# One-hot sorting of token slots in f32 from the unsplit x, with unrolled experts and a third up-projection buffer

## The reference

```python
gate = jnp.sum(jax.nn.one_hot(e_idx, N_EXPERTS, dtype=jnp.float32) * w[..., None], axis=1).astype(x.dtype)
y = jnp.zeros_like(t)
for e in range(N_EXPERTS):
    h = jax.nn.silu(t @ w_gate[e]) * (t @ w_up[e])
    y = y + gate[:, e:e + 1] * (h @ w_down[e])
```

## Time and profile before

| | |
|---|---|
| median of 3 runs | 1006.26 us (1005.80 to 1006.55) |
| profiled execution, own time | 1011.19 us |
| its span, first to last instruction | 1009.4 us |
| mean granted clock of PE | 0.903 of full speed |
| PE busy | 809.6 us, 80% of the span |
| DVE, ACT, POOL busy | 343.1, 199.6, 57.4 us |
| read from HBM | 249.46 MB |

### The profile page before, as it was taken

How to read it: one execution, slowest core, us unless ns; L and a number is a source line. 1 busy time by engine, 2 the same in 40 slices (tenths; PEclk the granted TensorE clock), 3 DMA queues, 4 the chain that set the end, 5 groups by cost and what they waited for, 6 DMA issues and landing times.

```text
span 1009.4 us, 10730 instructions
## 1 busy us (share of the span) xinstructions
PE 809.6 (80%) x4044; PEld 409.5 (41%) x4048; DVE 343.1 (34%) x744; ACT 199.6 (20%) x477; POOL 57.4 (6%) x54
## 2 busy tenths in 40 slices
PE   6989999938897877878799997697499878777750
PEld 4656777435432222222344865455343222222210
DVE  1033444376122212122540137536722222121228
ACT  1213334140211101011210036612221111010111
POOL 1020000040000000000200000002300000000010
PEclk9987999958999999999989997798599999999985
DMA  9641009340599999999693643234055999999942
GB/s 361 195 149 84 1 1 410 133 167 20 193 398 425 429 427 425 430 425 424 228 405 109 238 195 139 74 136 167 1 209 233 428 426 430 426 425 428 424 158 89
DMA packets 41303, 264.02 MB, mean 262 GB/s; under 512 B 6168, under 2 KB 10974, under 8 KB 23600
## 3 DMA queue, kind: packets, MB, share of 16 engines
q1 hardware_dynamic: 32032, 243.95, 58.9%
q0 software_dynamic: 3328, 10.51, 3.5%
q10 hardware_dynamic: 5904, 9.04, 2.5%
HBM read 249.46 MB, written 14.01 MB: 261 GB/s over the span
## 4 chain that ended last, share of the span: by engine, by line
PE 50%; DMA 27%; DVE 12%; SPq 6%; ACT 3%; issue 2%; POOL 0%; ACTq 0%; DVEq 0%; POOLq 0%
DMA arena<-in_expert_w_up 25%; PE bank L824 15%; PE bank L766 5%; PE bank L1061 4%; PE bank L1076 3%; PE bank L838 3%; PE bank L817 3%; SPq L435 2%; PE bank L754 2%; PE bank L702 2%; PE bank L617 1%; DVE arena L1635 1%; PE bank L747 1%; DVE arena L1798 1%; PE bank L680 1%
## 5 line engine op out<-in xcount | busy, mean ns | idle before, releaser
L824 PE MATMUL bank<-arena 128*64 128x512 f32 x1024 | 246.9, 638 | 64.1 <-DMA arena<-in_expert_w_up 59.6
L824 PEld LDWEIGHTS bank<-arena 128*64 128x64 f32 x1024 | 77.8, 145 | 230.3 <-issue 187.2
L1723 DVE COPY arena<-bank 128x256 f32<-128x256 f32 x32 | 13.6, 425 | 350.2 <-PE bank L831 350.2
L838 PE MATMUL bank<-arena 128*64 128x512 f32 x512 | 116.9, 598 | 17.0 <-DVE arena L1723 17.0
L1269 ACT ACTIVATE arena<-bank 128x256 f32<-128x256 f32 x32 | 12.3, 384 | 286.6 <-PE bank L824 286.6
L838 PEld LDWEIGHTS bank<-arena 128*64 128x64 f32 x512 | 34.1, 136 | 77.7 <-issue 59.3
L1716 DVE RECIPROCAL arena<-arena 128x256 f32<-128x256 f32 x32 | 56.1, 1754 | 1.1
L766 PE MATMUL bank<-arena 128*128 128x512 f32 x128 | 55.4, 593 | 1.3 <-ACT arena L1135 1.3
L1061 PE MATMUL bank<-arena 128*128 128x512 f32 x96 | 43.7, 616 | 1.7 <-issue 0.9
L1295 ACT COPY arena<-bank 128x512 f32<-128x512 f32 x32 | 18.8, 587 | 110.1 <-PE bank L838 110.1
L610 PE MATMUL bank<-arena 128*128 128x128 f32 (+1 forms) x144 | 24.5, 334 | 16.4 <-DVE arena L1635 8.1
(11 more groups left out here) (253 smaller groups left out, 929.2 us busy)
## 6 DMA issues: line engine op xcount, KB each, us to landing
arena<-in_expert_w_gate SPq DMA_DIRECT2D x32, 2048.0 KB, 16.7
arena<-in_expert_w_up SPq DMA_DIRECT2D x32, 2048.0 KB, 21.2
arena<-in_expert_w_down SPq DMA_DIRECT2D x64, 1024.0 KB, 20.4
arena<-in_w_out SPq DMA_DIRECT2D x4, 2048.0 KB, 9.9
expert_rows<-arena ACTq DMA_DIRECT2D x64, 128.0 KB, 7.6
arena<-in_w_kv_shared SPq DMA_DIRECT2D x3, 2048.0 KB, 10.4
arena<-in_w_mem_kv SPq DMA_DIRECT2D x2, 2048.0 KB, 16.5
arena<-in_w_in_b SPq DMA_DIRECT2D x2, 2048.0 KB, 20.3
```

Source lines behind the costliest of these rows:

```text
L824: last = mm(bank[j][64 * half:64 * half + 64, :].rearrange("p (u f) -> p u f", u=2), slots[:, k, 0:CAP], w[:, :, k, 256 * half:256 * half ...
L838: last = mm(bank[3 + j][64 * n:64 * n + 64, :], hid_t[:, j, c, 64 * half:64 * half + 64], dn[j][:, half, c, 512 * n:512 * n + 512], start= ...
```

## The change

- `x_part`, `x_stack`, `x_rest`, `x_mid`, the rounding on ACT and the six subtractions on POOL go. POOL keeps one memset of the tail of `xs`.
- DVE makes two f32 one-hot matrices. `pick` (128 columns) holds experts 0 and 1, made from each token's place within those two experts right after the counts are copied. `sort_pick` (576 columns) holds all slots and is made later in the chain, as `pick` was.
- `pack_first` sorts the slots of experts 0 and 1: 24 f32 matmuls of 128 columns (eight blocks, three token tiles). ACT copies them straight into `xg`, and up 0 and up 1 follow each other.
- `turn_rows` sorts all 576 slots in nine turns over three banks: eight turns of 512 columns (three f32 matmuls each) and a ninth with the last 64 columns of all eight blocks (24 matmuls). Four turns stand between down 0 and down 1, five between down 1 and up 2. ACT copies the even turns out, DVE the odd ones.
- The three up buffers rotate, so U(e+3) is issued when up e is done; D(e+1) is issued when down e-1 is done.
- The loops over experts are written out. `keep_warm` before the sort goes from 1536 columns to 512.

```diff
@@ -218,19 +218,15 @@
-        x_part = zm.cut(3 * D).bitcast(BF16).rearrange("p (s t d) -> p s t d", s=3, t=2)
-        x_stack = zm.cut(D // 2).bitcast(BF16)
-        ln2_par = Region(part_at).cut(2, D)
+        sort_pick = zm.cut(3, PACK)
+        zm.cut(3 * D - 3 * PACK)
+        pick = zm.cut(3, 2 * CAP)
...
+        ups = [gu[0], gu_one, gu[1]]
...
@@ -478,34 +481,24 @@
+                load_up(l, 2, ups[2], up_in[2])
+                for e in range(NE):
+                    if e + 3 < NE:
+                        sp.wait_ge(up_done, NE * l + e + 1)
+                        load_up(l, e + 3, ups[e % 3], up_in[e % 3])
+                    if 1 <= e < NE - 1:
+                        sp.wait_ge(down_done, NE * l + e)
+                        load_down(l, e + 1, (e + 1) % 2, dn_in[(e + 1) % 2])
...
+            def pack_first(l):
+
+                for half in range(2):
+                    b = bank[5 + half]
+                    for k in range(4):
+                        for t, (a, n) in enumerate(TOKS):
+                            last = mm(b[:, 2 * CAP * k:2 * CAP * (k + 1)], x_tok[0:n, t, 4 * half + k::KC], pick[0:n, t, :],
+                                      start=t == 0, stop=t == 2)
+                    last.then_inc(packed, 1)
+
+            def turn_rows(l, which):
+
+                for i in which:
+                    if i == 0:
+                        pe.wait_ge(sort_ready, l + 1)
+                    if i < 3:
+                        pe.wait_ge(pack_taken, 2 * (l + 1))
+                    else:
+                        pe.wait_ge(*turn_taken(l, i - 3))
+                    b = bank[5 + i % 3]
+                    for k in range(1 if i < KC else KC):
+                        for t, (a, n) in enumerate(TOKS):
+                            if i < KC:
+                                last = mm(b[:, :], x_tok[0:n, t, i::KC], sort_pick[0:n, t, 0:512], start=t == 0, stop=t == 2)
+                            else:
+                                last = mm(b[:, CAP * k:CAP * (k + 1)], x_tok[0:n, t, k::KC], sort_pick[0:n, t, 512:PACK],
+                                          start=t == 0, stop=t == 2)
+                    last.then_inc(rows_turned, 1)
...
-                keep_warm(bank[1], 1536)
...
+                keep_warm(bank[1], 512)
+                pe.wait_ge(pick_ready, l + 1)
+                pack_first(l)
+                up(0)
+                up(1)
+                down(0)
+                turn_rows(l, range(FIRST_TURNS))
+                down(1)
+                turn_rows(l, range(FIRST_TURNS, TURNS))
+                up(2)
+                for e in range(3, NE):
+                    up(e)
+                    down(e - 1)
+                down(NE - 1)
...
@@ -1273,61 +1267,66 @@
+                for half in range(2):
+                    ac.wait_ge(packed, 2 * l + half + 1)
+                    for j in range(2):
+                        last = nc.scalar.copy(xg[:, j, 4 * half:4 * half + 4, :],
+                                              bank[5 + half][:, :].rearrange("p (k s) -> p k s", k=4)[:, :, CAP * j:CAP * (j + 1)])
+                        own(last, pack_taken if j else None)
+                gate(0)
+                gate(1)
+                store(0)
+                take_rows(range(FIRST_TURNS))
+                store(1)
+                take_rows(range(FIRST_TURNS, TURNS))
...
+                for i in (TURNS - 2, TURNS - 1):
+                    ac.wait_ge(*turn_taken(l, i))
+                take(2)
+                take(3)
+                gate(2)
+                take(4)
...
@@ -1679,7 +1661,13 @@
+                    out_of(V.tensor_copy(counts[:, 3 * NE:4 * NE], b[:, 3 * NE:4 * NE]))
+                own.settle()
+                for t, (a, n) in enumerate(TOKS):
+                    for e in range(2):
+                        c = NE * t + e
+                        own(ts(pick[0:n, t, CAP * e:CAP * (e + 1)], cst("iota")[0:n, 0:CAP], counts[0:n, c:c + 1],
+                               sel_any[0:n, c:c + 1], ALU.is_equal, ALU.mult), pick_ready if (t, e) == (2, 1) else None)
...
+                form(0)
+                turned(0)
+                form(1)
+                take_rows(range(FIRST_TURNS))
+                turned(1)
+                take_rows(range(FIRST_TURNS, TURNS))
+                form(2)
...
@@ -1888,28 +1884,14 @@
-                        own(G.tensor_tensor(r, x_tok[:, t, :], x_part[:, 0, t, :], ALU.subtract), rest_ready)
...
+                own(G.memset(xs[:, :, PACK:XGW], 0.0), tail_ready)
+                po.wait_ge(rows_turned, TURNS * (l + 1))
                 ln_load(ln2_par, "ln2_g", "ln2_b", l)
```

## The result

The median is 1077.67 us (1070.87 to 1082.83, 4 runs) against 1006.40 for the kernel before in the same comparison: a ratio of 1.0683, 95% interval 1.0589 to 1.0776. The prediction had 1018.0 in a range of 1007 to 1026. So the direction was right and the size was not: 71 us for 12. The profiled execution took 1082.04 us, its span 1080.2.

What follows compares the result with a forecast made beforehand. The weight stream bounds the mixture, with a hole before it and PE's tail after. A 7.5 us earlier start a layer, less a longer hole and tail, sums to +11.7 us: 1006.26 becomes 1018.0 us, range 1007 to 1026.

Steps and rivals of the forecast that it cites:

- the price of the sorts' records: pack_first, ninth turn: 0.11 us a record at full clock; wide turns: 0.433 us a record, 10.4 us for four turns.
- the 0.5 us that the prediction had allowed for the clock: In pack_first: 0.5 us added because PE's clock may rise later, within 6.4 us in all.
- The 32-row records: In turn_rows: a third of the wide records, with 32 rows only, priced in full like 128-row ones.
- narrow records leave PE at 1.2 GHz: Rival, chance 0.07: pack_first costs 4.2 us more, the ninth turn 5.3, time 1037 us.
- The wide f32 records are cheaper: Rival in turn_rows: under 0.433 us, at 0.22 each 997.6 us; chance 0.12 with other shortenings of PE's way to U5.
- the 32-row records cost in proportion: Rival in turn_rows, chance 0.08: 5.2 us less a layer, 1007.6 us, no change that can be told.
- The contention: POOL's subtractions slow three DVE operations between x and the ranks; removing them saves 7.48 us per layer.
- D3 behind U5: On SP's queue: D3 waits behind up 2 and U5 until about 295 us, though down 1 has long been done.
- the stream itself: Weight loads: U5 lands 12.8 us after its issue, U15 153.5 us later, an expert every 15.35 us.
- D13 behind U15: Layer's end: down 13 waits for D13, landing at 466.5 us, and stands before up 15; PE ends at 488.15.
- The passing of all delay before U5 to the end: Mixture's end is the start of gapless loads, plus loads still to come, plus PE's tail.
- the new order with its third buffer: Weight loads: the third buffer moves one U ahead of the hole and no D, leaving 11 U and 13 D.

Runs made afterwards that it cites:

- e5: Changed kernel with both edits: sorts read neighbouring columns of x and the third tile uses all 128 rows; 1028.88 us, ratio 1.0188.
- e1: Changed kernel with sorts reading 128 neighbouring columns of x instead of every eighth; 1055.89 us, ratio 1.0483.
- e2: Changed kernel with the third tile of x used with all 128 rows, the extra rows meeting zeros; 1052.50 us, ratio 1.0398.
- e12: Changed kernel with keep_warm ahead of the first sort at 1536 columns instead of 512; 1076.45 us, one execution.
- e3: Changed kernel with D3 issued on SP's queue before the wait for up 2 and U5; 1070.66 us, ratio 1.0591.
- e4: Changed kernel with the ninth turn doing only its first of eight feature groups (6 records for 48); 1054.19 us, ratio 1.0422.
- e6: Changed kernel with sorts back in three bf16 parts, its order of work and three up buffers kept; 1022.01 us, ratio 1.0113.
- e7: e6 with SP issuing each D before the U of its step from expert 2 on; 1005.67 us, ratio 0.9977.
- e8: e7 with x in two bf16 parts, the third left out; 1006.33 us, ratio 0.9943.

## Why the prediction was right in direction and wrong in size

**The step that failed is the price of the sorts' records**: "Four such records take 0.44 us at full clock, 0.11 each", used for pack_first and the ninth turn, and in a smaller way "64 such records take 27.72 us, 0.433 each" for the turns. Both rows have a stationary of 128 rows that reads neighbouring columns, and the first is of transposes (L680). The change's records read every eighth f32 and change between 128 and 32 rows. Measured in the changed kernel: 0.328 us in pack_first, 0.30 in the ninth turn and 0.537 in the wide turns. Per layer that is 9.9 us in pack_first, 9.1 in the ninth and 2 x 2.5 in the turns, and with the half clock that follows 2.3 in up 0 and up 1 and some 1.6 from the ninth turn to U5. Less the 0.5 us that the prediction had allowed for the clock, that is 27.4 us, against the 27.3 by which U5 was late. From there to PE's end 3.4 more were lost, and layer 0 ends at 518.86 for 488.15. e5, which takes the two causes away, puts these terms of layer 0 back to their predicted values, but for the last: from the ninth turn's end to U5 it takes 11.2 us for 10.2, since up 2 takes 8.8 us for 7.95.

Of the two causes, a wide turn of 3.22 us goes to 2.97 without the stride, 2.66 without the row changes and 2.63 without both. So in the turns the row change is the cost, and the stride makes it dearer (0.56 for 0.34 us a turn). In the narrow sorts both count. By the starts of single records at full clock, a neighbouring one with equal rows comes every 0.11 us (e5), with the row changes every 0.18 (e1's pack_first); a strided one every 0.24 (e2) and 0.29 (e12). At half clock the plain record takes 0.21 (e5's first five), the strided one with equal rows 0.24 as before.

**The 32-row records** I priced in full, and L610's row was the reason. That row is of transposes of equal rows in sequence; it does not show a change of rows within a group. The sentence of the Trainium skill that I put beside it (TensorE: Matmul & The Clock Gate, "Why this matters for your kernels") speaks of one record alone, and these runs do not contradict it.

**The rival "narrow records leave PE at 1.2 GHz"** had 0.07 and 1037 us. The clock did fall in both narrow sorts, but as a consequence: a longer busy stretch ahead does not keep it (e12, one execution), and without the slow records (e5) it did not fall within them. Its price, 0.22 a record, holds for plain records at half clock (0.21) and was too low for these. "The wide f32 records are cheaper" and "the 32-row records cost in proportion" did not happen.

**What held.** The contention: from the last logits to the ranks it takes 10.5 us for 16.3, the 5.8 that L1651 and L1653 were to give, and in all the ranks end 7.6 us earlier for 7.48. (The POOL row lies inside L1651 only; beside L1653 stands the next subtraction, L1899, from 224.26 on for 2.13 us.) D3 behind U5 (e3). From U5's issue onward the stream itself: by its DMA rows U5 landed 13.5 us after its issue, and U15 154.6 us later, for 12.8 and 153.5. D13 behind U15 with up 15 after it: PE's tail is 28.3 us for 26.75, though the half clock fell on down 13 and not on up 15. The passing of all delay before U5 to the end (e4). And the new order with its third buffer bought nothing: with the old format it is slower by 1.1% (e6), and with the queue's order changed too it is level with the kernel before (e7).

**What the edited sorts leave open.** e5's median is 10.9 us above 1018.0, and above the range; against the kernel before's 1008.67 in its own comparison it is 20.2 us slower for the predicted 11.7. In its profile layer 0 ends where predicted, layer 1's mixture takes 2.8 us more, and the stretch between them 240.5 us where the saved contention should have left some 234.7. No edit touches that stretch's attention, and the changed kernel had 235.5 there. The windows of layer 1's attention, from the first record of L680 to the first of L710, in the changed kernel and in e5:

```profile
639.60:678.25 38.65, 28.65 (x212) 19.81 (x214) 27.90 (x79) 28.58 (x114) 0.00 (x0) 0.87 0.30 124
```

```profile
608.38:652.57 44.19, 37.01 (x212) 26.02 (x214) 27.90 (x79) 28.77 (x114) 0.00 (x0) 0.65 0.25 106
```

The same 212 records ran at a granted clock of 0.87 and of 0.65, and the stretch takes 5.5 us more. So this part of the excess is the clock in the attention, not the sorts. Why it fell earlier there no run shows, and the 2.8 us of layer 1's mixture stay open.

## What to carry to other kernels

A price for a record holds only for its whole form: besides columns and type, compare the stride with which the stationary is read and the row counts of the records before and after it, and look at the weight loads' own group before taking a matmul row as a price. Pad a ragged last tile to the full rows, or stack it as the bf16 kernel did to 96, rather than alternate 128 and 32. Where a transfer stream is the bound, everything between it and the gate of its next load counts one for one (e4), so issue what is already free before waiting for what is not.

## What was not expected of the hardware

- In f32 matmuls a stationary read with a stride of eight loads in 314 to 335 ns, whether the granted clock is 1.00 or 0.50. One of neighbouring columns takes 188 to 192 at 1.00 and 316 to 322 at 0.50 (e1's ninth turn by its single loads, and the rank matmuls, L808). One of bf16 with the stride takes 156, and f32 transposes with it (L610) 180 to 231.
- A change of the stationary's rows between 128 and 32 costs 0.34 us a turn with neighbouring columns and 0.56 with the stride, two changes in each, with no load running for 0.63 us before each change in the changed kernel; in bf16 a change to 64 rows made a record of 0.22 us into 0.37, and one to 96 rows cost nothing.
- Fewer records on PE came with a lower granted clock: e8, with five records for e7's seven, was at 0.50 from 226 to 236 us where e7 had 0.76, and gave part of its gain back in up 0 and up 1 (16.03 for 13.96 us).
- Gate and up weights in pieces of 2 KB for 16 KB cost 6% of the stream (400 for 426 GB/s).
